# A fused transformer layer on one core: a later square, a later token tile, earlier folds and a reordered bias step

## The chip, the core and the metric

The kernel runs on one core of a Trainium2 chip. Its time is the device time of one execution in microseconds (us). The core's engines are TensorE (PE, matmuls), VectorE (DVE), ScalarE (ACT), GpSimd (POOL) and SyncE (SP, which here only issues DMAs). Each works through its own list of instructions in order and waits on semaphores that the others raise. An instruction that waits holds up all that stand behind it on its engine. ACT also issues DMAs, and these stand in its list between its other instructions.

## The reference

One layer, 1024 tokens of width 1024, all float32:

```
mod = silu(c) @ w_ada + b_ada;  shift1, scale1, gate1, shift2, scale2, gate2 = split(mod, 6)
h = rmsnorm(x, norm1_gain) * (1 + scale1) + shift1
q, k, v, p = split(h @ w_in)                       # 512 | 128 | 128 | 512 columns
attn = sliding_window_attention(q, k, v)           # chunks of 64, window 128, sinks, T5 bias, QK-norm
pool = multiscale_pool(p)                          # causal means over 2, 4, 8, 16 tokens, then a linear map
merged = concat(rmsnorm(attn) * g_a, rmsnorm(pool) * g_p)
x = x + gate1 * (merged @ w_out)
h2 = rmsnorm(x, norm2_gain) * (1 + scale2) + shift2
x = x + gate2 * ((silu(h2 @ w_gate) * (h2 @ w_up)) @ w_down)
```

## The kernel before

Every large product keeps float32 accuracy by splitting both factors into a rounded high part (made by ACT) and a low part (made by DVE): three matmuls stand for one, `mm3` at L2173 to L2175. Tokens lie in eight tiles of 128 (t = 0 to 7), the width in eight blocks of 128 (j = 0 to 7).

**Start.** DVE forms the first modulation vectors from rows of `w_ada`, one instruction of 128x1024 for each block j (L1404): eight columns of `scale1`, eight of `shift1`. ACT makes the gain column from each scale column, then the high parts of the tokens (`h_high_block`) and of `w_in` (`wi_high`); DVE makes the low parts (`h_low_block`, `wi_low`); PE multiplies tiles 0 and 1 with block j (`project_block`). The shift enters as a bias row: ACT and DVE split each shift column (`shift_high` L765, `shift_low` L1553), PE multiplies it with `w_in` (`shift_part`, L2232 and L2233), ACT copies the three finished rows (`shift_row` L780), PE spreads them over 128 partitions (`shift_rows` L2242), and ACT copies them to SBUF (`keep_shift` L785). `evac_q`, `evac_kv` and `evac_p` on DVE (L1564, L1574, L1583) add them to every tile's projections, so nothing of tile 0 leaves PSUM before.

Among these steps ACT squares the token tiles for the RMS norm (`square_x`, L734). Tile t + 1 is loaded into the same buffer `x_st` after the square of tile t, so each square waits for a load of 512 KB. `constants` issues eight small loads on ACT's queue (the bias tiles' source, pool weights, sinks).

**Loop.** `for it in range(NT + 2)` stands on each engine. In turn `it`, PE projects tile `it`, scores belong to tile `it - 1`, and the attention output to tile `it - 2`. A tile from t = 2 on needs `scale_x` (L1534), `h_high` (L746, ACT) and `h_low` (L1541) before its projection.

**Background.** The vectors gate1, scale2 and shift2 come from 24 pieces of 512 KB of `w_ada` (eight for each). SP loads them into a ring of four buffers (`stage`), which lie on the buffers of shift blocks 4 to 7. DVE takes each with one instruction, a fold: L1414 and L1417 for gate1, L1404 for the others. `FOLDS` gives the number for each turn; the ring is refilled as folds end (`ada_used`). `TAKEN` names the turn in which a finished vector is used. The order on each engine is the order of the code; no planner moves it.

After the loop's turns come the output projection and the gated FFN, which no line of the change touches.

Of the kernel before, what the change touches and what calls it, by code (L numbers as in the profile page):

```python
# [26 lines left out]
P = 128  # L27
# [32 lines left out]
def build_program(nc, x, c, w_ada, b_ada, norm1_gain, w_in, q_gain, k_gain, attn_sinks, rel_bias_table,  # L60
                  w_pool, pool_scale, attn_out_gain, pool_out_gain, w_out, norm2_gain, w_gate, w_up,
                  w_down, identity, onehot, inv_count, xt, w_adat, out):
    SEQ, D = x.shape[1], x.shape[2]
    NT = SEQ // P
    KT = D // P
# [11 lines left out]
    RING = 4  # L77
# [10 lines left out]
    with ExitStack() as ctx:  # L88
# [143 lines left out]
        def bank(b):  # L232
            return ps[:, b, :]
# [18 lines left out]
        FOLDS = (3, 4, 4, 5, 4, 4, 0, 0)  # L252
        SCALED = ((), (), (), (), (), (0, 1), (2, 3, 4), (5,), (6, 7))
        TAKEN = {3: GATE1, 4: SCALE2, 6: SHIFT2}
# [243 lines left out]
        def _(sp):  # L498
# [33 lines left out]
            sp.dma_start(g1bc[:, :], b_ada[0, GATE1 * D:(GATE1 + 1) * D].partition_broadcast(P)).then_inc(gate_in, 16)  # L532
            sp.dma_start(g2bc[:, :], b_ada[0, GATE2 * D:(GATE2 + 1) * D].partition_broadcast(P)).then_inc(gate_in, 16)
            sp.wait_ge(hlo_done, KT + 1)
            load_xt(3)
            sp.wait_ge(shift_sum, KT)
            for n, (mm, k) in enumerate(pieces):
                if n >= RING:
                    sp.wait_ge(ada_used, n - RING + 1)
                src = wa_d[k * P:(k + 1) * P, mm * D:(mm + 1) * D] if mm == GATE1 else wat_d[mm * D + k * P:mm * D + (k + 1) * P, :]  # L540
                sp.dma_start(piece_view(n), src).then_inc(stage_in[n % RING], 16)
                if (mm, k) == (GATE1, KT - 1):
                    for j in range(KT // 2):
                        sp.dma_start(wo_raw[:, j, :], wout_d[j * P:(j + 1) * P, :]).then_inc(wo_in[0], 16)
# [141 lines left out]
        def _(act):  # L686
# [122 lines left out]
            shift_high(KT - 4)  # L809
            shift_high(KT - 3)  # L810
            square_x(1)
            for j in range(KT - 2, KT):
                shift_high(j)
            h_high(2)
            constants()
# [49 lines left out]
            for it in range(NT + 2):  # L865
# [65 lines left out]
                if it == 0:  # L931
                    h_high(3)
# [20 lines left out]
                if it + 2 < NT:  # L953
                    square_x(it + 2)
                if 1 <= it and it + 3 < NT:
                    load_xt(it + 3)
# [429 lines left out]
        def _(dve):  # L1386
# [231 lines left out]
            for it in range(NT + 2):  # L1618
# [9 lines left out]
                if it == 0:  # L1628
                    h_low(2)
                    scale_x(3)  # L1630
                    evac_q(0)
# [36 lines left out]
                if it == 0:  # L1668
                    fold(0)
# [35 lines left out]
                if it == 0:  # L1705
                    evac_p(0)
                    dve.wait_ge(wpl_done, 1)
                    evac_q(1)
                    evac_kv(1)
                    bias_tiles()  # L1710
                    h_low(3)
                    fold(1)
# [17 lines left out]
                if 1 <= it < NT - 1:  # L1730
                    evac_q(it + 1)
                if it < NT:
                    for n in range(sum(FOLDS[:it]) if it else 2, sum(FOLDS[:it + 1])):
                        fold(n)
                    if it < NT - 1:
                        scale_wo(it)
# [433 lines left out]
        def _(pe):  # L2170
# [19 lines left out]

            pe.wait_ge(vrow_in, 16 * 2)
# [52 lines left out]
            def project_first():  # L2244

                for j in range(KT - 1):
                    project_block(0, j)
                    project_block(1, j)
                    if j == 1:
                        small_vectors()  # L2250
                    if j >= 4:
                        if j == 4:
                            pe.wait_ge(vcol_done, 2)
                            pe.wait_ge(rel_done, 1)
                        for part in range(3):
                            shift_part(part, (j - 4,))
                project_block(0, KT - 1)
                project_block(1, KT - 1, (1,))
# [5 lines left out]
                project_block(1, KT - 1, (0, 2))  # L2264
# [420 lines left out]
```

## Time and profile before

| | us |
|---|---|
| median of 3 runs | 962.2 (962.1 to 962.76) |
| the profiled execution | 962.17 |
| its span, first to last instruction | 960.4 |
| PE busy, of the span | 925.4 (96%) |
| DVE busy | 789.3 (82%) |
| ACT busy | 521.0 (54%) |
| POOL busy | 283.8 (30%) |

The page lists for each engine the time in which it works. The chain of waits is followed back from the last instruction, at each step to what let it start. A timeline row gives an instruction's start and length, and in brackets the idle time of the engine before it with what ended that. The busy share is a mean over very different stages, so the stages are read one by one.

### The profile page before, as it was taken

The page shows a single profiled execution, that of the slowest core. Times are in us where ns is not written, and L with a number is a line of the kernel's source. Part 1 is how long each engine was busy: PE and PEld are TensorE (multiplying, and loading weights), DVE is VectorE, ACT ScalarE, POOL GpSimd, SP SyncE. Part 2 cuts the span into 40 slices and gives each one's busy share as a digit, 9 for nine tenths or more (in the row PEclk, how much of TensorE's full clock was granted, in tenths as well). Part 3 has the DMA queues.
Part 4 walks back from the last instruction along what each step waited for, and adds up shares of the span by engine and source line. Part 5 has one row for each costly group of instructions (what it writes and reads, how often), then busy time and mean ns, then how long its engine had stood idle before and what let it go on. Part 6 is the DMA issues. An engine that isn't in the chain of part 4 may idle for free.

```text
span 960.4 us, 14014 instructions
## 1 busy us (share of the span) xinstructions
PE 925.4 (96%) x4327; PEld 760.3 (79%) x4327; DVE 789.3 (82%) x1239; ACT 521.0 (54%) x1006; POOL 283.8 (30%) x243
## 2 busy tenths in 40 slices
PE   7988999989999998999999999999999999999998
PEld 6647788778887777888888888888888888888886
DVE  4949999999689968888787977879698787977797
ACT  4544655576345645555464654646465464655543
POOL 0025455432100100703306061240704215070334
PEclk9999999999999999999999999999999999999999
DMA  9965754338345495557456556644656556455624
GB/s 359 390 214 158 281 176 154 110 122 274 132 129 179 142 328 209 197 202 259 152 195 227 210 178 218 220 173 175 227 198 231 196 186 229 175 183 210 219 88 176
DMA packets 96135, 193.97 MB, mean 202 GB/s; under 512 B 6512, under 2 KB 57440, under 8 KB 96096
## 3 DMA queue, kind: packets, MB, share of 16 engines
q1 hardware_dynamic: 90816, 182.05, 54.2%
q10 hardware_dynamic: 5280, 11.45, 3.3%
q8 instruction: 19, 0.31, 0.1%
q14 instruction: 20, 0.16, 0.1%
HBM read 176.30 MB, written 17.17 MB: 201 GB/s over the span
## 4 chain that ended last, share of the span: by engine, by line
PE 71%; DVE 17%; issue 4%; DMA 3%; ACT 3%; POOL 1%; SPq 1%; ACTq 0%; DVEq 0%; POOLq 0%
PE ps L2173 23%; PE ps L2174 23%; PE ps L2175 23%; DVE stage L1404 2%; DMA raw_u<-in_w_up 1%; DVE wo_raw L1500 1%; DVE ada_in_raw L1404 1%; DMA x_st<-in_x 1%; DVE nmax L1645 1%; DMA wi_raw<-in_w_in 1%; DVE acc L1417 1%; DVE s_sb L1644 1%; DVE wi_lo L1588 1%; DVE wo_lo L1505 1%; PE ps L2426 1%
## 5 line engine op out<-in xcount | busy, mean ns | idle before, releaser
L1348 POOL TENSOR_TENSOR x<-x,p1s 128x512 f32<-128x512 f32 x80 | 117.0, 1483 | 422.4 <-ACT p1s L1045 421.6
L2173 PE MATMUL ps<-bs,ring 128*128 128x512 f32 x344 | 134.2, 390 | 3.3 <-ACT ps L973 2.6
L2175 PE MATMUL ps<-bs,ring 128*128 128x512 f32 x344 | 133.9, 389 | 0.0
L2174 PE MATMUL ps<-bs,ring 128*128 128x512 f32 x344 | 133.8, 389 | 0.0
L1787 DVE TENSOR_TENSOR ring<-s,ring 128x512 fp32r<-128x512 f32 x88 | 68.7, 799 | 50.0 <-ACT ring L966 50.0
L2173 PE MATMUL ps<-h_hi,ring 128*128 128x512 f32 x272 | 106.1, 390 | 0.6 <-DVE h_lo L1780 0.6
L2174 PE MATMUL ps<-h_lo,ring 128*128 128x512 f32 x272 | 105.8, 389 | 0.0
L2175 PE MATMUL ps<-h_hi,ring 128*128 128x512 f32 x272 | 105.8, 389 | 0.0
L966 ACT ACTIVATE ring<-s 128x512 fp32r<-128x512 f32 x88 | 53.8, 623 | 66.5 <-PE ps L2175 66.5
L2173 PEld LDWEIGHTS ps<-bs,ring 128*128 128x128 f32 x344 | 64.6, 188 | 18.1 <-issue 3.4
L2173 PE MATMUL ps<-wi_hi,ht_hi 128*128 128x512 f32 (+1 forms) x192 | 71.0, 370 | 7.9 <-DVE ht_lo L1547 2.3
L2175 PEld LDWEIGHTS ps<-bs,ring 128*128 128x128 f32 x344 | 64.6, 188 | 13.4
L2174 PEld LDWEIGHTS ps<-bs,ring 128*128 128x128 f32 x344 | 64.6, 188 | 13.3
L2174 PE MATMUL ps<-wi_lo,ht_hi 128*128 128x512 f32 (+1 forms) x192 | 68.7, 358 | 0.0
L2175 PE MATMUL ps<-wi_hi,ht_lo 128*128 128x512 f32 (+1 forms) x192 | 68.5, 357 | 0.0
L2173 PEld LDWEIGHTS ps<-h_hi,ring 128*128 128x128 f32 x272 | 51.1, 188 | 11.5 <-DVE h_lo L1780 1.0
L2175 PEld LDWEIGHTS ps<-h_hi,ring 128*128 128x128 f32 x272 | 51.1, 188 | 10.6
L2174 PEld LDWEIGHTS ps<-h_lo,ring 128*128 128x128 f32 x272 | 51.1, 188 | 10.5
L2173 PE MATMUL ps<-wo_hi,h_hi 128*128 128x512 f32 x128 | 51.3, 401 | 0.8 <-DVE x L1526 0.5
L2174 PE MATMUL ps<-t_lo_d,h_hi 128*128 128x512 f32 x132 | 51.4, 389 | 0.0
L1845 DVE TENSOR_TENSOR x<-x,ps 128x512 f32<-128x512 f32 x40 | 26.4, 681 | 29.4 <-PE ps L2175 29.4
L2173 PEld LDWEIGHTS ps<-wi_hi,ht_hi 128*128 128x128 f32 x192 | 36.8, 191 | 17.1 <-issue 5.0
(302 smaller groups left out, 2344.2 us busy)
## 6 DMA issues: line engine op xcount, KB each, us to landing
bs<-bs_scratch SPq DMA_DIRECT2D x166, 512.0 KB, 6.2
raw_g<-in_w_gate SPq DMA_DIRECT2D x11, 1024.0 KB, 5.3
raw_u<-in_w_up SPq DMA_DIRECT2D x11, 1024.0 KB, 7.7
raw_d<-in_w_down SPq DMA_DIRECT2D x20, 512.0 KB, 4.2
ada_in_raw<-in_w_adat SPq DMA_DIRECT2D x16, 512.0 KB, 11.1
stage<-in_w_adat SPq DMA_DIRECT2D x16, 512.0 KB, 5.7
wi_raw<-in_w_in SPq DMA_DIRECT2D x8, 640.0 KB, 12.3
stage<-in_w_ada SPq DMA_DIRECT2D x8, 512.0 KB, 4.6
```

The source lines that it names most:

```text
L966: act.activation(ring[m][(par + pos(p, o)) % 2][:, 0], a_source(m, o), ACT.Copy).then_inc(a_hi, 1)
L1348: pool.tensor_tensor(x1_half(t, 1), x1_half(t, 1), p1s[j][:, :], ALU.add).then_inc(pool_evac, 1)
L1404: return dve.scalar_tensor_tensor(out=piece, in0=piece, scalar=1.0, in1=row, op0=ALU.mult, op1=ALU.mult, accum_out=mod_sum[:, v, j:j + 1])
L1417: ins = dve.scalar_tensor_tensor(out=acc[:, :], in0=piece_view(n), scalar=cact[:, 0, k:k + 1], in1=acc[:, :], op0=ALU.mult, op1=ALU.add)
L1500: dve.scalar_tensor_tensor(out=wo_raw[:, k, :], in0=wo_raw[:, k, :], scalar=gmix[:, k:k + 1], in1=g1bc[:, :], op0=ALU.mult, op1=ALU.mult). ...
L1505: dve.tensor_tensor(wo_lo[:, k, :], wo_raw[:, k, :], wo_hi_row(k).bitcast(F32), ALU.subtract).then_inc(wo_lo_done, 1)
L1588: dve.tensor_tensor(wi_lo[:, j, cols], wi_raw[:, j, cols], wi_hi[:, j, cols].bitcast(F32), ALU.subtract).then_inc(wi_lo_done, 1)
L1787: dve.tensor_tensor(r[:, 1], a_source(m, o), r[:, 0].bitcast(F32), ALU.subtract).then_inc(a_lo, 1)
L1845: dve.tensor_tensor(c, c, bank(XB[j]), ALU.add).then_inc(down_evac, 1)
L2173: pe.matmul(dst, s_hi, m_hi, start=start, stop=False, skip_group_check=onto)
L2174: pe.matmul(dst, s_hi, m_lo, start=False, stop=False, skip_group_check=onto)
L2175: return pe.matmul(dst, s_lo, m_hi, start=False, stop=stop, skip_group_check=onto)
```

## The change

- ACT squares tile 1 after the last four shift columns and after `h_high(2)`, ahead of `constants`; before, it stood between shift columns 5 and 6.
- The low and high parts of tile 3 are made in turn 1 and not in turn 0: `scale_x(3)` and `h_low(3)` on DVE stand around turn 1's folds, `h_high(3)` on ACT behind turn 1's `square_x(3)`.
- Three gate1 folds stand ahead of `evac_q(0)`; before, one stood behind the `v` copies of turn 0 and two between the bias tiles and the first scores. Turn 1 has three folds instead of four, turn 5 has five instead of four, and scale2 is taken in turn 5.
- SP loads piece n (0 to 3) as soon as shift column 4 + n is done; before, all four waited for column 7. The two gate rows `g1bc` and `g2bc` are loaded after the first fold and not ahead of token tile 3.
- PE fills its wait after block 0 with eight matmuls on a matrix of ones, into a bank that nobody reads then. The last k and v block of tile 1 stands behind the shift products and not ahead of them.

```diff
-        FOLDS = (3, 4, 4, 5, 4, 4, 0, 0)
+        FOLDS = (3, 3, 4, 5, 4, 5, 0, 0)
-        TAKEN = {3: GATE1, 4: SCALE2, 6: SHIFT2}
+        TAKEN = {3: GATE1, 5: SCALE2, 6: SHIFT2}
...
             load_xt(2)
-            sp.dma_start(g1bc[:, :], b_ada[0, GATE1 * D:(GATE1 + 1) * D].partition_broadcast(P)).then_inc(gate_in, 16)
-            sp.dma_start(g2bc[:, :], b_ada[0, GATE2 * D:(GATE2 + 1) * D].partition_broadcast(P)).then_inc(gate_in, 16)
             sp.wait_ge(hlo_done, KT + 1)
             load_xt(3)
-            sp.wait_ge(shift_sum, KT)
             for n, (mm, k) in enumerate(pieces):
-                if n >= RING:
+                if n < RING:
+                    sp.wait_ge(shift_sum, KT - RING + n + 1)
+                else:
                     sp.wait_ge(ada_used, n - RING + 1)
+                if n == RING:
+                    for bc, gate in ((g1bc, GATE1), (g2bc, GATE2)):
+                        sp.dma_start(bc[:, :], b_ada[0, gate * D:(gate + 1) * D].partition_broadcast(P)).then_inc(gate_in, 16)
...
             square_x(0)
-            shift_high(KT - 4)
-            shift_high(KT - 3)
-            square_x(1)
-            for j in range(KT - 2, KT):
+            for j in range(KT - 4, KT):
                 shift_high(j)
             h_high(2)
+            square_x(1)
             constants()
...
-                if it == 0:
-                    h_high(3)
...
                 if it + 2 < NT:
                     square_x(it + 2)
+                if it == 1:
+                    h_high(3)
...
                 if it == 0:
                     h_low(2)
-                    scale_x(3)
+                    fold(0)
+                    fold(1)
+                    fold(2)
                     evac_q(0)
...
-                if it == 0:
-                    fold(0)
...
                     bias_tiles()
-                    h_low(3)
-                    fold(1)
...
                     evac_q(it + 1)
+                if it == 1:
+                    scale_x(3)
                 if it < NT:
-                    for n in range(sum(FOLDS[:it]) if it else 2, sum(FOLDS[:it + 1])):
+                    for n in range(sum(FOLDS[:it]) if it else 3, sum(FOLDS[:it + 1])):
                         fold(n)
+                    if it == 1:
+                        h_low(3)
...
+            def keep_busy_gap(n):
+                for _ in range(n):
+                    pe.matmul(bank(6)[:, 0:P], ones[:, :], ones[:, :], start=True, stop=True)
...
                     project_block(1, j)
+                    if j == 0:
+                        keep_busy_gap(8)
...
                 project_block(0, KT - 1)
-                project_block(1, KT - 1, (1,))
                 for j in (KT - 5, KT - 4):
...
-                project_block(1, KT - 1, (0, 2))
+                project_block(1, KT - 1, (1, 0, 2))
```

ACT, end of the start phase, before: the squares (`x_st,ssx`), the shift columns (`sh`) and the high part of tile 2 (`ht_hi<-sq_m`), up to the first copied shift row.

```order
L734 ACTIVATE x_st,ssx<-x_st 128x1024
L737 DMA x_st<-in_x 128x1024
L765 ACTIVATE sh<-mod_sum,vcol 128x1 x2
L734 ACTIVATE x_st,ssx<-x_st 128x1024
L737 DMA x_st<-in_x 128x1024
L765 ACTIVATE sh<-mod_sum,vcol 128x1 x2
L746 ACTIVATE ht_hi<-sq_m 128x1024
L718 DMA bias<-rel_scratch 64x4x128 x2
```

The same place of the changed kernel, whose line numbers are two higher.

```order
L736 ACTIVATE x_st,ssx<-x_st 128x1024
L739 DMA x_st<-in_x 128x1024
L767 ACTIVATE sh<-mod_sum,vcol 128x1 x4
L748 ACTIVATE ht_hi<-sq_m 128x1024
L736 ACTIVATE x_st,ssx<-x_st 128x1024
L739 DMA x_st<-in_x 128x1024
L720 DMA bias<-rel_scratch 64x4x128 x2
```

The second square now stands behind four shift columns and behind tile 2's high part; it still stands ahead of the constants and of every shift row.

ACT, from turn 1 to turn 2, changed kernel: the exponentials and square of turn 1, the high part of tile 3 (`ht_hi<-xs`), then turn 2's copies of pool output (`mT`), probabilities (`pt_sb`) and queries (`qbd`).

```order
L841 ACTIVATE sinkex<-sinkin 128x4
L736 ACTIVATE x_st,ssx<-x_st 128x1024
L739 DMA x_st<-in_x 128x1024
L748 ACTIVATE ht_hi<-xs 128x1024
L743 DMA xs<-in_xt 128x1024
L879 ACTIVATE mT<-ps 128x512
L821 ACTIVATE pt_sb<-ps 128x512 x2
L898 ACTIVATE qbd<-ps,vcol 64x8x64 x2
```

The row `ht_hi<-xs` is new here; before, it stood in turn 0 behind the square of q and k, so all of turn 2 now stands behind it.

DVE, end of turn 1, as a piece of the difference: tile 2's q leaves PSUM (L1564), then the folds into `acc`, then k and v of tile 2 (L1574) and the next scores.

```order
 L1583 SCALAR_TENSOR_TENSOR p_sb<-ps,rsx,bp 128x512
 L1564 SCALAR_TENSOR_TENSOR qkv<-ps,rsx,bqkv 128x512
-L1417 SCALAR_TENSOR_TENSOR acc<-stage,cact,acc 128x1024 x4
+L1534 TENSOR_TENSOR xs<-xs,a 128x1024
+L1417 SCALAR_TENSOR_TENSOR acc<-stage,cact,acc 128x1024 x3
+L1541 TENSOR_TENSOR ht_lo<-xs,ht_hi 128x1024
 L1574 SCALAR_TENSOR_TENSOR qkv<-ps,rsx,bqkv 128x256
```

Two instructions on tile 3 come in around the folds, and one fold leaves.

## Rows read from the trace of the kernel before

**Rows 1.** The chain of waits, shares of the span by engine

```profile
PE 71%; DVE 17%; issue 4%; DMA 3%; ACT 3%; POOL 1%; SPq 1%; ACTq 0%; DVEq 0%; POOLq 0%
```

**Rows 2.** By stage: length, busy PE, PEld, DVE, ACT, POOL, PE clock, DMA share, GB/s

```profile
16.30:19.00 2.70, 2.69 (x8) 2.30 (x9) 1.71 (x4) 1.53 (x3) 0.00 (x0) 0.50 1.01 409
...
30.00:45.00 15.00, 14.62 (x76) 10.86 (x75) 15.00 (x26) 8.41 (x15) 1.85 (x2) 1.00 1.01 381
...
75.00:195.00 120.00, 110.10 (x640) 94.44 (x640) 116.39 (x236) 71.53 (x204) 59.25 (x57) 0.99 0.52 176
...
400.00:800.00 400.00, 400.00 (x1766) 331.20 (x1765) 320.68 (x464) 218.59 (x379) 121.44 (x86) 1.00 0.57 204
```

**Rows 3.** Timeline (start us, length us, [idle before]) of PE, block 1 of tiles 0, 1

```profile
16.32 0.79 PE L2173 MATMUL ps<-wi_hi,ht_hi 128*128 128x512 f32 x1 [2.33 <-DVE ht_lo L1547]
...
19.63 0.39 PE L2173 MATMUL ps<-wi_hi,ht_hi 128*128 128x512 f32 x1
...
21.45 0.23 PE L2206 MATMUL ps<-ident,mT 18*128 18x18 f32 x1
```

**Rows 4.** Timeline of DVE, start phase

```profile
24.34 0.48 DVE L1547 SCALAR_TENSOR_TENSOR ht_lo<-xs,a,ht_hi 128x256 fp32r<-128x256 f32 x1 [2.91 <-ACT ht_hi L761]
...
37.27 1.23 DVE L1404 SCALAR_TENSOR_TENSOR ada_in_raw<-ada_in_raw,crow 128x1024 f32<-128x1024 f32 x1
...
46.72 1.23 DVE L1404 SCALAR_TENSOR_TENSOR ada_in_raw<-ada_in_raw,crow 128x1024 f32<-128x1024 f32 x1
...
52.34 0.22 DVE L1553 SCALAR_TENSOR_TENSOR sh<-mod_sum,vcol,sh 128x1 fp32r<-128x1 f32 x1 [4.38 <-ACT sh L765]
...
61.22 0.75 DVE L1564 SCALAR_TENSOR_TENSOR qkv<-ps,rsx,bqkv 128x512 f32<-128x512 f32 x1 [4.05 <-ACT bqkv L785]
```

**Rows 5.** DMA issued at 20.42: size, us to landing

```profile
ada_in_raw<-in_w_adat SPq DMA_DIRECT2D x1, 512.0 KB, 15.4
```

**Rows 6.** Timeline of ACT, end of the start phase (ACTq: its DMA issues)

```profile
50.43 1.06 ACT L734 ACTIVATE x_st<-x_st 128x1024 f32<-128x1024 f32 x1 [4.70 <-DMA x_st<-in_x]
...
52.01 0.67 ACT L765 ACTIVATE sh<-mod_sum,vcol 128x1 fp32r<-128x1 f32 x2 [0.43 <-ACT x_st L734]
53.73 1.06 ACT L746 ACTIVATE ht_hi<-sq_m 128x1024 fp32r<-128x1024 f32 x1 [1.05 <-DVE sq_m L1534]
...
56.88 1.31 ACTq L727 DMA_DIRECT2D sinks<-in_attn_sinks  x2
58.24 0.59 ACT L780 ACTIVATE shrow_q<-ps 2x512 f32<-2x512 f32 x1 [3.46 <-PE ps L2233]
```

**Rows 7.** Timeline of PE: shift products, shift rows, scores of tiles 0 and 1

```profile
53.88 0.59 PE L2232 MATMUL ps<-wi_hi,sh 128*2 128x512 f32 x1 [0.64 <-DVE sh L1553]
...
59.34 1.12 PE L2242 MATMUL ps<-shrow_q,ones 2*128 2x512 f32 x2
...
71.95 1.95 PE L2400 MATMUL ps<-kT,qbd 128*128 128x128 f32 x16
...
91.69 2.02 PE L2400 MATMUL ps<-kT,qbd 128*128 128x128 f32 x16 [1.10 <-ACT kT L848]
```

**Rows 8.** Timeline of DVE, turns 0 and 1

```profile
71.36 2.08 DVE L1541 TENSOR_TENSOR ht_lo<-xs,ht_hi 128x1024 fp32r<-128x1024 f32 x1
73.37 3.50 DVE L1417 SCALAR_TENSOR_TENSOR acc<-stage,cact,acc 128x1024 f32<-128x1024 f32 x2
76.80 0.68 DVE L1644 TENSOR_TENSOR s_sb<-ps,bias 128x512 f32<-128x512 f32 x1
...
88.22 6.14 DVE L1417 SCALAR_TENSOR_TENSOR acc<-stage,cact,acc 128x1024 f32<-128x1024 f32 x4
...
94.67 0.68 DVE L1644 TENSOR_TENSOR s_sb<-ps,bias 128x512 f32<-128x512 f32 x1
```

**Rows 9.** Timeline of ACT, the first copy of turn 2

```profile
85.78 0.60 ACT L879 ACTIVATE mT<-ps 128x512 f32<-128x512 f32 x1 [2.66 <-PE ps L2300]
```

**Rows 10.** Timeline of POOL, the pool weights

```profile
67.92 1.27 POOL L1332 TENSOR_TENSOR wpl<-wpl,pt_sb 128x512 f32<-128x512 f32 x1
```

## The prediction

> **What bounds the kernel now.** I read the chain of waits first. Over the span it is 71% PE and 17% DVE [rows 1], so the question is which stages are DVE's. The busy time by stage tells: from 400 to 800 us PE works all 400.00 us, while from 30 to 45 DVE works 15.00 of 15.00 and from 75 to 195 it works 116.39 of 120 against PE's 110.10 [rows 2]. The reader is to see that the change lies wholly in DVE's stages. What DVE gains there before the loop ends starts PE's long stage sooner by as much; nothing behind it is touched. The timelines then show three places where DVE waits or is late.
>
> - PE comes to block 1 at 16.32 after 2.33 us idle and runs it at half its clock: the granted clock is 0.50 from 16.3 to 19.0 [rows 2, 3]. DVE waits 2.91 at 24.34 for what follows from that block [rows 4].
> - DVE has formed the last shift column at 46.72 + 1.23 = 47.95, and then waits 4.38 for ACT's shift column 6, which stands behind the square of tile 1, which waited 4.70 for its load [rows 4, 6]. DVE waits 4.05 more for the bias row, until 61.22 [rows 4].
> - The first scores are ready on PE from 71.95, but DVE adds their bias only at 76.80, behind the low part of tile 3 and two folds [rows 7, 8].
>
> All times below count from the start of the trace before. Its execution took 962.17, that is the span of 960.4 and 1.8 around it, and lies 0.03 under the median of 962.2.
>
> **A, the eight filling matmuls (gain 1.4).** Nine matmuls of tile 0 took 19.63 - 16.32 = 3.31 us at half clock. The same nine of tile 1, at full clock, took 21.45 - 19.63 = 1.82 with the small wait behind them [rows 3]. So 1.5 is to be had. The eight become 16 instructions of the form of the scores, which take 1.95 / 16 = 0.12 each [rows 7]: 1.95 of the 2.33 idle, 0.4 left. At half clock they would take 3.9 and make the block 1.6 late; the blocks ahead of the gap had no such wait, so I count this a rival and not a bound. From block 1 the way goes over ACT's small vectors to DVE's 24.34, and DVE has no idle time from 30 to 45 [rows 2], so the gain reaches 47.95. One load limits it: the scale column of block 7 was issued at 20.42, landed 15.4 later at 35.8 and was used at 37.27 [rows 4, 5]. That leaves 1.4. Bounds: 0 and 1.5.
>
> **B, the square behind the shift columns (gain 2.2).** Without the wait for the load, shift column 6 can be split at 47.95. Before, tile 2's high part on ACT began 53.73 - 52.34 = 1.39 after that [rows 4, 6], so now at 49.3; it ends at 50.4. The square of tile 1 finds its load at 50.43, as before, and with its accumulator read and the next load's issue takes 52.01 - 50.43 = 1.6 [rows 6]. The constants' issues take from 53.73 to 56.88 + 1.31 = 58.19, 4.5 us [rows 6], so they end at 56.5, and the shift row's copy, 0.59, ends at 57.1. On PE the shift products can now run through from about 49.5; what lay between 53.88 and 59.34 takes at most 5.5, so PE is done by 55 and waits 2.1. ACT, with the square and the constants ahead of the row, is what is late next. PE spread the row at 59.34 [rows 7], now at 57.1. B keeps A only if the square's load also comes 1.4 sooner. It is issued 1.4 sooner, and the two gate rows, 1 MB or 2.6 us at the 409 GB/s of the start [rows 2], are no longer ahead of it, so I take A whole. Bounds: 1.1, if PE spreads the first row at half clock (1.12 more), and 2.5. The k and v block behind the shift products costs nothing, since PE has 2 us to spare there.
>
> **C, the folds and tile 3 out of the way of the first scores (gain 3.9).** From `evac_q(0)` to the scores on PE it is 71.95 - 61.22 = 10.7 us, and half of the 16 score matmuls, 1.0, make the first chunk. DVE came 76.80 - 61.22 = 15.6 after `evac_q(0)` [rows 4, 7, 8]. Now 11.7: 3.9 sooner. DVE no longer ends this stretch, PE does. Bounds: 0 and the 2.08 + 3.50 = 5.6 that leave DVE [rows 8]. The three folds lie in the wait before `evac_q(0)`: low part of tile 2 until about 51.7, then 0.75 + 2 x 1.23, by 55.0, against an `evac_q(0)` at 59.0 without A. Their pieces are issued when shift columns 4 to 6 end, by 46.72 at the latest [rows 4]; with the 8 us that the square's load took they are there by 54.7, so even the last leaves 3 us. `scale_x(3)`, 1.2, leaves the same wait, which is why it counts below.
>
> **D, tile 3 in turn 1 (loss 2.75).** This is the price. `h_high(3)` on ACT stands ahead of all copies of turn 2, and waits for `scale_x(3)`, which stands on DVE behind `evac_q(2)`. That ended at 88.22; DVE's next scores began at 94.67, 6.45 later [rows 8]. Now: `scale_x(3)` 1.2, `h_high(3)` 1.06, then turn 2's chain over ACT and PE from the `mT` copy to the scores, 91.69 - 85.78 = 5.9 [rows 7, 9], and 1.0 for the first chunk: 9.2. DVE's own work in that time, one scale, three folds and a low part, 5 x 1.23 = 6.2, lies within it. Loss 9.2 - 6.45 = 2.75. Bounds: 1.9, if the copies of the probabilities no longer wait for PE, and 4.2, if all PE work of the chain runs at half clock.
>
> DVE's own 6.2 stands on 1.23 for each [rows 4]. Before, beside POOL's window sums, the four folds took 6.14, 1.53 each, and the low part of tile 3 took 2.08 [rows 8]; five at 2.08 would be 10.4, past the 9.2, and the loss 4.0. I take 1.23, because POOL's sums of tile 1 start only after ACT's copy of its projection, which is now behind the five.
>
> By the Trainium skill, page "SBUF — State Buffer", section "SBUF: two separate sides", a VectorE instruction with two SBUF inputs and a GpSimd instruction that reads SBUF lock each other out of a shared port. By that rule the loss is 2.75, since POOL has nothing to do then; by the mean of 1.53, taken for these forms everywhere, it would be the same, and only at 2.08 each 4.0. The trace agrees with the rule in so far as these forms are slow only beside POOL.
>
> **E, the fifth fold in turn 5 (loss 1.25).** One fold of 1.23 more where DVE is full [rows 2]; beside POOL up to 2.1 [rows 8]. The scale2 step only moves from turn 4 to 5.
>
> **At no cost:** the earlier pieces (SP waits for shift columns instead of the last one, and its next item was piece 0 anyway) and the later gate rows, first used in turn 3.
>
> Sum: 1.4 + 2.2 + 3.9 - 2.75 - 1.25 = 3.5, so 962.17 - 3.5 = **958.7**. Likely own range 957.8 to 959.9.
>
> **The rivals.**
>
> *PE loses its clock.* PE idles 2.1 us ahead of the shift row, and in turn 2 the `mT` copy comes 88.22 + 2.26 = 90.5 instead of 85.78, so PE waits 4.7 more there. After 2.33 idle PE was slow at 16.32, and after a wait of 0.64 that followed another one it was slow at 53.88 [rows 3, 7]. Against it: the first of the new idles is shorter than 2.33. Price: B 1.1 less and D 1.45 more, 961.2.
>
> *The loads on ACT's queue come late.* The gate rows and pieces 4 to 6 now fall on the time of the constants. POOL scaled the pool weights at 67.92 without waiting for them [rows 10]; POOL and the constants' issue both come some 3.5 sooner, so they meet as before unless the DMAs are slower. The gate rows alone are 2.6 us of DMA time; between none and all of that is lost, 1.5 as a middle: 960.2, at worst 961.3. By the Trainium skill, page "DMA: Bandwidth & Descriptors", section "Queues, rings and completion order", each DMA engine takes packets in turn from the queues that have work for it, so that SP's loads slow ACT's; by that rule this rival is the likelier. The square's load, for which ACT waited 4.70, fits it [rows 6].
>
> *The fillers don't hold the clock.* A is 0: 960.1. Little speaks for it; the idle left is 0.4.
>
> *More than the sum.* D lies at its lower bound, 1.9, and the fifth fold falls into a wait of DVE in turn 5, so E is 0: 956.6. For it, DVE is busy 116.39 of 120, not all [rows 2]; against it, those 3.6 are split over six turns.
>
> *Slower: ACT's queue holds turn 2.* The other terms make 6.25, so the gain is gone once the stretch after `evac_q(2)` takes 6.45 + 6.25 = 12.7. That needs PE to fall behind DVE too: right after the scores PE projects tile 3's q, 24 matmuls of about 0.23 or 5.5 us, and if turn 2's copies have to wait for all of that, 9.2 + 5.5 = 14.7 make the kernel 2.0 slower: 964.2. Against it: PE is idle 9.9 us from 75 to 195 and can catch up [rows 2].
>
> **How the numbers follow.** Forecast 0.60, clock 0.12, late loads 0.10, fillers 0.05, more 0.08, slower 0.05. What a measurement of this kernel can tell from no change is about 0.2%, 1.9 us. Faster, under 960.3: forecast, more, fillers and half of the late loads are 0.78, less 0.03 for the forecast's own tail: 0.75. Within: clock, the other half of the loads, and 0.02 of that tail: 0.19. Slower: 0.06. The range, 957.1 to 961.3, takes in clock, loads and fillers, and leaves out the slower case and most of the case of more.
>
> **What would show it.** A: the granted clock stays at 1 from 16 to 20 and DVE's 24.34 becomes 22.9. B: no idle of DVE before the second part of shift column 6, and the shift row's copy directly behind the constants. C: first bias add within 1.2 us of the first scores. D: an idle time of about 3 us on DVE before the second tile's scores, ended by PE, behind ACT's `h_high(3)`. E: five folds in turn 5, DVE without idle. The prediction is wrong if the gain up to the first scores, 7.5 us, is not there, or if DVE's wait in turn 2 is under 1 or over 5 us.

## The result, and the profile after

| | before | changed |
|---|---|---|
| median of 11 runs each, us | 961.86 (960.78 to 962.76) | 966.17 (962.49 to 967.02) |
| ratio, 95% interval | | 1.0035 [1.0023, 1.0048] |
| the profiled execution, its span, us | 962.17, 960.4 | 962.49, 960.7 |

The changed kernel is 0.35% slower by the ratio, which is estimated over all runs of both; the two medians lie 0.45% apart. Forecast was 958.7, with a range up to 961.3. The profiled execution is the fastest of the changed kernel's eleven, so this trace shows less than the whole loss; the experiments bring a second one nearer the median.

The chain of waits by engine, which answers to [rows 1]:

```profile
PE 78%; DVE 12%; DMA 4%; ACT 3%; issue 2%; ACTq 1%; SPq 0%; POOL 0%; DVEq 0%; POOLq 0%
```

PE has seven points more and DVE five fewer. The stages of the same trace, columns as in [rows 2]:

```profile
13.60:18.00 4.40, 3.96 (x27) 3.46 (x27) 3.03 (x4) 2.05 (x5) 0.00 (x0) 1.00 1.01 412
...
52.00:56.00 4.00, 1.34 (x6) 0.75 (x4) 1.84 (x2) 0.00 (x0) 0.00 (x0) 1.00 0.91 275
56.00:60.00 4.00, 2.12 (x5) 1.24 (x6) 0.00 (x0) 1.92 (x4) 0.00 (x0) 0.83 1.03 338
60.00:64.00 4.00, 4.00 (x8) 2.05 (x7) 2.04 (x4) 2.54 (x5) 0.00 (x0) 0.50 1.04 374
...
84.00:88.00 4.00, 0.04 (x1) 0.07 (x2) 3.90 (x4) 2.21 (x4) 0.00 (x0) 0.74 0.30 80
88.00:92.00 4.00, 4.00 (x15) 3.53 (x16) 3.16 (x4) 2.62 (x5) 0.77 (x2) 0.50 0.89 308
184.00:188.00 4.00, 2.70 (x6) 2.17 (x7) 3.86 (x8) 2.81 (x15) 0.21 (x1) 0.62 0.00 0
400.00:800.00 400.00, 400.00 (x1767) 331.16 (x1765) 320.12 (x464) 218.41 (x378) 122.19 (x85) 1.00 0.58 205
```

The long stage is as it was. The granted clock (the last column but two; 1.00 is 2.4 GHz, 0.50 is 1.2) is 1.00 where it had been 0.50, at block 1. Three places show the lower level: around 60, from 88 and around 185. Only the third has no counterpart in the kernel before, whose clock is 1.00 there. The first two are longer than what stood there before, of which these are the rows:

```profile
52.00:56.00 4.00, 2.74 (x11) 1.06 (x12) 2.67 (x5) 1.65 (x3) 0.00 (x0) 0.71 1.01 392
56.00:60.00 4.00, 4.00 (x15) 2.06 (x14) 1.18 (x2) 1.33 (x3) 0.00 (x0) 0.86 0.93 241
...
84.00:88.00 4.00, 4.00 (x20) 3.70 (x21) 3.86 (x11) 1.71 (x3) 0.34 (x1) 0.57 0.73 262
```

In the changed kernel the first two stand right behind a stretch in which PE hardly worked. PE's timeline shows the waits (columns as in [rows 3]); it answers to [rows 3] and [rows 7]:

```profile
13.66 1.95 PE L2195 MATMUL ps<-ones 128*128 128x128 f32 x16
16.04 0.50 PE L2175 MATMUL ps<-wi_hi,ht_hi 128*128 128x512 f32 x1 [0.44 <-DVE ht_lo L1547]
...
57.88 1.36 PE L2248 MATMUL ps<-shrow_q,ones 2*128 2x512 f32 x2 [4.54 <-ACT shrow_q L782]
59.05 2.76 PE L2248 MATMUL ps<-shrow_kp,ones 2*128 2x256 f32 x4
...
71.86 2.02 PE L2407 MATMUL ps<-kT,qbd 128*128 128x128 f32 x16
...
87.96 1.09 PE L2360 MATMUL ps<-ident,qn 128*128 128x128 f32 x4 [4.95 <-ACT pt_sb L821]
...
93.21 2.02 PE L2407 MATMUL ps<-kT,qbd 128*128 128x128 f32 x16
```

What PE waits for is ACT, both times. ACT's timeline, which answers to [rows 6] and [rows 9]:

```profile
50.70 1.36 ACTq L720 DMA_DIRECT2D bias<-rel_scratch  x2
52.11 1.01 ACTq L723 DMA_DIRECT2D pt_sb<-in_inv_count  x1
53.15 0.60 ACTq L724 DMA_DIRECT2D wpl<-in_w_pool  x1
53.78 2.04 ACTq L725 DMA_DIRECT2D pt_sb<-in_pool_scale  x1
55.85 1.35 ACTq L729 DMA_DIRECT2D sinks<-in_attn_sinks  x2
57.25 0.59 ACT L782 ACTIVATE shrow_q<-ps 2x512 f32<-2x512 f32 x1 [6.97 <-issue]
...
61.85 0.60 ACT L787 ACTIVATE bp<-ps 128x512 f32<-128x512 f32 x1 [1.32 <-PE ps L2248]
62.34 0.73 ACT L775 ACTIVATE sq_qk<-qkv 128x640 f32<-128x640 f32 x1
...
85.79 1.06 ACT L748 ACTIVATE ht_hi<-xs 128x1024 fp32r<-128x1024 f32 x1 [6.34 <-DVE xs L1534]
...
86.75 0.58 ACT L879 ACTIVATE mT<-ps 128x512 f32<-128x512 f32 x1
```

The constants' issues took 6.50 us (50.70 to 57.20); the forecast took 4.5 from [rows 6]. In turn 2 ACT stands 6.34 us for tile 3. DVE's timeline, which answers to [rows 4] and [rows 8]:

```profile
22.63 0.48 DVE L1547 SCALAR_TENSOR_TENSOR ht_lo<-xs,a,ht_hi 128x256 fp32r<-128x256 f32 x1 [1.47 <-ACT ht_hi L763]
...
45.65 1.22 DVE L1404 SCALAR_TENSOR_TENSOR ada_in_raw<-ada_in_raw,crow 128x1024 f32<-128x1024 f32 x1
...
60.01 0.75 DVE L1564 SCALAR_TENSOR_TENSOR qkv<-ps,rsx,bqkv 128x512 f32<-128x512 f32 x1 [6.07 <-ACT bqkv L787]
...
73.09 0.69 DVE L1646 TENSOR_TENSOR s_sb<-ps,bias 128x512 f32<-128x512 f32 x1 [1.89 <-PE ps L2407]
...
83.88 0.74 DVE L1564 SCALAR_TENSOR_TENSOR qkv<-ps,rsx,bqkv 128x512 f32<-128x512 f32 x1
...
94.37 0.69 DVE L1646 TENSOR_TENSOR s_sb<-ps,bias 128x512 f32<-128x512 f32 x1 [3.11 <-PE ps L2407]
```

It is ahead of the kernel before by 1.07 at the last shift column, 1.2 at the first q, 3.7 at the first bias add, and 0.3 at the second. So the forecast's 7.5 up to the first scores is half missing, and turn 2 takes what came.

### The profile page after: what moved, and what is told of

Read it like the earlier page. It is cut to its first block, busy times and chain, and to the rows that moved or that the text cites. A ratio compares the mean times of both kernels' runs of the same rounds, so it can differ in the third digit from the quotient of the medians.

```text
span 960.7 us, 14046 instructions
## 1 busy us (share of the span) xinstructions
PE 928.3 (97%) x4343; PEld 763.5 (79%) x4343; DVE 785.4 (82%) x1239; ACT 520.6 (54%) x1006; POOL 277.5 (29%) x243
## 4 chain that ended last, share of the span: by engine, by line
PE 78%; DVE 12%; DMA 4%; ACT 3%; issue 2%; ACTq 1%; SPq 0%; POOL 0%; DVEq 0%; POOLq 0%
PE ps L2175 25%; PE ps L2177 24%; PE ps L2176 24%; DMA ada_in_raw<-in_w_adat 2%; DMA raw_u<-in_w_up 1%; DVE stage L1404 1%; DVE ada_in_raw L1404 1%; PE ps L2296 1%; PE ps L2407 1%; DMA wi_raw<-in_w_in 1%; DVE wo_lo L1505 1%; PE ps L2433 1%; ACT ht_hi L748 0%; DVE xs L1534 0%; DVE wi_lo L1588 0%
## 5 line engine op out<-in xcount | busy, mean ns | idle before, releaser
L2176 PEld LDWEIGHTS ps<-bs,ring 128*128 128x128 f32 x344 | 64.6, 188 | 13.1
L2177 PE MATMUL ps<-wo_hi,h_lo 128*128 128x512 f32 x128 | 50.0, 390 | 0.0
```

Source lines behind the costliest of these rows:

```text
L2176: pe.matmul(dst, s_hi, m_lo, start=False, stop=False, skip_group_check=onto)
L2177: return pe.matmul(dst, s_lo, m_hi, start=False, stop=stop, skip_group_check=onto)
```

## The experiments

My theory after this: ACT's queue holds PE twice. The constants' issues stretch because the loads that the early folds release fall on them, and tile 3's high part holds turn 2; behind each wait PE runs at the lower clock. Rivals: the gate rows stretch the issues, turn 2 or the fifth fold alone decides, the clock at the start is paid back later. Ratios are to runs of the kernel before on the same chip, so variants from different chips are compared by their ratios; that of the changed kernel is 1.0035, and 1.0038 in e8.

### e1: the fillers alone

In the kernel before:

```diff
+                    if j == 0:
+                        keep_busy_gap(8)
```

> The kernel before with the eight filling matmuls alone (term A). If the fillers do what was forecast, the granted clock stays at 1 from 16 to 20 us, the last shift column ends 1.1 to 1.4 us sooner (46.6 to 46.9 instead of 47.95), and of that at most 1.4 is left at the end: 960.5 to 961.9. If the gain is lost because the shift row still stands behind the square and its load, the time is that of the kernel before within 0.3. If a full clock at the start is paid for by a fall of the granted clock later (the rival), a new stretch at 0.50 shows after 50 us and the time is above 963.

Measured: 959.86 against 961.18, ratio 0.9989 [0.9981, 0.9998]. A gain of about 1.1 (0.2 to 1.8), so A is real by the times. The profiled execution took 961.63, 1.8 above the median, and in it the gain does not pass the shift row. The last shift column ends at 46.59, 1.36 sooner, but the load of the second square, issued 1.36 sooner, lands only 0.2 sooner, so the shift row's copy is 0.26 sooner (57.98). PE then ran the shift products at the lower clock for longer: the granted clock is 0.88, 0.50 and 0.76 in the windows from 48 to 60, against 1.00, 0.71 and 0.86 before. The first q comes at 61.50, no sooner than before. So the second of the expectation's cases is what this trace shows; no stretch at the lower clock is new, but this one is longer.

### e2: tile 3's scale and high part back in turn 0

```diff
+                    scale_x(3)
                     evac_q(0)
...
-                if it == 1:
-                    scale_x(3)
...
+                if it == 0:
+                    h_high(3)
...
-                if it == 1:
-                    h_high(3)
```

> The changed kernel with tile 3's scale and high part back in turn 0 (the scale behind the three folds in the wait for the shift row, the high part on ACT behind the first square of q and k); its low part stays in turn 1 behind the folds. If ACT's wait for tile 3 is what holds turn 2 (term D and the half clock behind it), ACT's copies of turn 2 start at the end of evac of q of tile 2, PE's idle of about 5 us from 83 to 88 and the 0.50 from 88 to 92 are gone, and the kernel is 3 to 4 us faster than the changed one: 962 to 963. If PE's late start in turn 2 has another cause (the rival: DVE's folds and low part), PE is idle there as before and the gain is under 1 us.

Measured: 962.56, ratio 1.0013 [1.0002, 1.0025]: the time is in the expected band, but by the ratios the gain over the changed kernel is 0.22%, about 2 us and not 3 to 4. From the q of tile 2 to the second bias add it takes 95.34 - 88.24 = 7.10; in the kernel before 94.67 - 87.56 = 7.11, in the changed one 94.37 - 83.88 = 10.49. The clock stays at 1.00 from 84 to 96. So tile 3's scale and high part, for which ACT waits, make the whole of D. But in this profile the issues took 8.1 us and PE waited 6.36 for the shift row.

### e3: the gate rows in their old place

```diff
             load_xt(2)
+            sp.dma_start(g1bc[:, :], b_ada[0, GATE1 * D:(GATE1 + 1) * D].partition_broadcast(P)).then_inc(gate_in, 16)
+            sp.dma_start(g2bc[:, :], b_ada[0, GATE2 * D:(GATE2 + 1) * D].partition_broadcast(P)).then_inc(gate_in, 16)
```

The same two lines are gone from the loop over the pieces.

> The changed kernel with the loads of the two gate rows back in their old place on SP's queue, ahead of tile 3's tokens. If it is these rows that stretch the issue of ACT's constants from 4.46 to 6.5 us, the issues take 4.5 again, the shift row's copy starts at about 55.2 instead of 57.25, PE's idle ahead of it is 2.5 instead of 4.54 us, and the kernel is 1 to 2 us faster than the changed one. If the pieces do it, or the square's load now waits for the gate rows, the shift row comes no sooner and the time is that of the changed kernel within 0.5.

Measured: 966.56, ratio 1.0060 [1.0046, 1.0075]. No gain. ACT's second square and its last issues in this run:

```profile
50.45 1.06 ACT L735 ACTIVATE x_st<-x_st 128x1024 f32<-128x1024 f32 x1 [1.42 <-DMA x_st<-in_x]
...
54.63 1.50 ACTq L724 DMA_DIRECT2D pt_sb<-in_pool_scale  x1
56.17 4.44 ACTq L728 DMA_DIRECT2D sinks<-in_attn_sinks  x2
60.66 0.59 ACT L781 ACTIVATE shrow_q<-ps 2x512 f32<-2x512 f32 x1 [9.06 <-issue]
```

With the gate rows gone from there the eight issues took 8.6 us, and the two for the sinks, 1 KB each, 4.44 instead of 1.31. So the gate rows are not needed for the stretch; whether they add to it in the changed kernel is not shown. The expectation's other case came too: behind the gate rows the square's load is late, the square starts at 50.45 instead of 49.15, and the issues at 52.02 instead of 50.70. So the later gate rows brought the square forward, as B had it.

### e4: the constants behind the kept shift rows

```diff
             square_x(1)
-            constants()
...
                     keep_shift(2)
+                    constants()
```

> The changed kernel with ACT's constants issued behind the three kept shift rows instead of ahead of the shift row's copy. If the issues on ACT's queue hold the shift row and the half clock behind PE's idle eats A and B, the copy starts when PE is done with the products (about 53.5 instead of 57.25), PE idles under 1.5 us, the granted clock from 56 to 68 is at least 0.9, DVE's first q comes at about 57 instead of 60.01, and the kernel is 3 to 4 us faster than the changed one, unless the pool weights or the bias tables then come late: in that case POOL's scaling of the weights (67.8) or DVE's bias tiles move back by 2 to 4 us and the gain is gone. If the idle there decides nothing (the rival: turn 2 decides), the time is that of the changed kernel within 1.

Measured: 964.31, ratio 1.0033 [1.0021, 1.0045]: by the ratio no gain over the changed kernel, which the expectation's exception and its rival both allow. The trace tells them apart. The first q came at 55.32, 4.7 sooner than in the changed kernel, but the second q at 69.30 instead of 69.10:

```profile
69.30 0.75 DVE L1564 SCALAR_TENSOR_TENSOR qkv<-ps,rsx,bqkv 128x512 f32<-128x512 f32 x1 [2.59 <-POOL wpl L1332]
```

POOL's weights take the place of the shift row, as the exception had it: the issues now stand ahead of `square_qk(0)`, and POOL waits 1.56 us for the last of these loads before it scales the weights at 68.00. One thing I did not expect: PE passed from the products to the rows at 53.44 with no wait over 0.4, and its clock fell all the same, to 0.50 from 57 to 60, which makes 0.62 of this stretch:

```profile
56.00:60.00 4.00, 3.78 (x10) 2.99 (x11) 0.47 (x2) 0.48 (x1) 0.00 (x0) 0.62 0.97 368
```

### e5: the later pieces wait for the shift rows

```diff
                 if n == RING:
+                    sp.wait_ge(shift_done, 3)
```

> The changed kernel with one wait more on SP's queue: the gate rows and the fourth and later GATE1 pieces are issued only when the shift rows are kept. If the loads that the early folds release are what stretches the issue of ACT's constants (6.5 us in the changed kernel, 8.1 and 8.6 in two of its variants, 4.4 to 4.5 with the old order), the issues take 4.5 us again and land in about 5 instead of 10, the shift row's copy starts at about 55.2, PE idles 2 to 2.5 us ahead of it as forecast in B, and the kernel is 2 to 4 us faster than the changed one: 962 to 964. If the first three pieces, loaded before 48 us, do it (the rival), the issues stay at 6 us or more and so does the time.

Measured: 961.41, ratio 0.9999 [0.9990, 1.0009]: the loss is gone with one wait, but the gain that was forecast is not there. ACT's timeline:

```profile
53.26 0.53 ACTq L726 DMA_DIRECT2D pt_sb<-in_pool_scale  x1
53.82 1.44 ACTq L730 DMA_DIRECT2D sinks<-in_attn_sinks  x2
55.31 0.59 ACT L783 ACTIVATE shrow_q<-ps 2x512 f32<-2x512 f32 x1 [5.00 <-issue]
```

The eight issues take 4.53 us (50.73 to 55.26) and the copy comes at 55.31. The loads too land sooner. The DMA view (KB each, median us to landing) has for the pool scale, first in the changed kernel, then here:

```profile
pt_sb<-in_pool_scale ACTq DMA_DIRECT2D x1, 256.0 KB, 11.1
```

```profile
pt_sb<-in_pool_scale ACTq DMA_DIRECT2D x1, 256.0 KB, 4.7
```

With e3, where the gate rows were gone and the issues stretched all the same, this points to the three pieces that the early folds release, 1.5 MB on SP's queue between 52 and 56.

### e6: the constants among the shift columns

```diff
-            for j in range(KT - 4, KT):
+            for j, loads in zip(range(KT - 4, KT), (bias_loads, pool_loads, scale_load, sink_loads)):
                 shift_high(j)
+                loads()
             h_high(2)
             square_x(1)
-            constants()
```

(the four functions are `constants` cut in parts)

> The changed kernel with the issues of ACT's constants put one or two at a time behind shift columns 4 to 7, in ACT's waits of about 1 us there, so that nothing but the second square stands ahead of the shift row. If ACT's issues are what holds the shift row, its copy starts when PE is done (53 to 54), PE has no idle there and keeps its clock, the constants land before 58 and hold nothing, and the kernel is 5 to 7 us faster than the changed one: 959 to 961. If the issues are stretched there too, the shift columns come late instead, by 2 us or more, and the gain is under 3. If turn 2 decides everything (the rival), the first scores come 5 us sooner and the time does not change.

Measured: 959.80, ratio 0.9982 [0.9973, 0.9991], 4.8 under the changed kernel on the same chip (e8). The copy of the shift row starts at 53.74 and PE waits 1.22 for it instead of 4.54; but the sinks' two issues, right behind SP's first four pieces, took 4.04 us and held `h_high(2)`:

```profile
47.07 4.04 ACTq L734 DMA_DIRECT2D sinks<-in_attn_sinks  x2
```

The time is the expected one, but not the "hold nothing": an issue is stretched there too, with none of the later pieces issued yet. PE did not keep its clock either: it is at 0.50 from 57 to 62, behind waits of 1.22 and 0.66.

### e7: the folds of the turns as before

```diff
-        FOLDS = (3, 3, 4, 5, 4, 5, 0, 0)
+        FOLDS = (3, 4, 4, 5, 4, 4, 0, 0)
-        TAKEN = {3: GATE1, 5: SCALE2, 6: SHIFT2}
+        TAKEN = {3: GATE1, 4: SCALE2, 6: SHIFT2}
```

> The changed kernel with the folds of the turns as before (four in turn 1 and four in turn 5, the scale2 step in turn 4); three stay in the wait for the shift row. If the fifth fold is what costs term E, the turn of tile 5 is 1.1 to 1.25 us shorter, and the stretch at a low granted clock from 184 to 192, which no trace with the old folds has, is gone with 0.5 to 1 us more: 964.2 to 964.8. The fourth fold of turn 1 lies in DVE's wait of 3.11 us there and costs nothing. If turn 5 has room (the rival), there is no gain; if DVE's work decides in turn 2, it is 1.2 us slower.

Measured: 963.26, ratio 1.0020 [1.0010, 1.0030], 1.4 under the changed kernel on the same chip (e8), with intervals that overlap. The stretch at the lower clock around 186 is gone:

```profile
184.00:188.00 4.00, 2.33 (x11) 1.61 (x10) 3.74 (x8) 3.13 (x12) 0.00 (x0) 1.00 0.01 2
```

That the new folds always bring this stretch is not so: e5, which has them, shows 1.00 from 172 to 196, although PE waits 2.43 us there as in the changed kernel (2.38).

### e8: the changed kernel once more

> The changed kernel once more, for a second profile. Its one profile so far is of its fastest run, 3.7 us under its median. If the run to run difference comes from the constants' issue, a profile of a run near the median shows these issues at 8 us or more instead of 6.5, the shift row's copy at 59 to 61 instead of 57.25 and the stretch at half clock behind it longer by about as much; if it comes from elsewhere, 57.25 stands and another place is late.

Measured: 964.63, ratio 1.0038 [1.0025, 1.0051]; the profiled execution took 964.58. Its ACT timeline:

```profile
53.36 1.50 ACTq L725 DMA_DIRECT2D pt_sb<-in_pool_scale  x1
54.89 3.06 ACTq L729 DMA_DIRECT2D sinks<-in_attn_sinks  x2
58.00 0.59 ACT L782 ACTIVATE shrow_q<-ps 2x512 f32<-2x512 f32 x1 [7.60 <-issue]
```

The issues took 7.1 us, under the 8 that I expected. The copy is 0.75 later than in the first profile, the first q 1.47 later (61.48), the second bias add 1.75 later (96.12) and the span 2.1 longer. So neither number of the expectation came, but the direction holds: 0.75 of the later first q is the issues, 0.7 the first row, which PE ran in 2.07 us instead of 1.36 at the lower clock, and 0.35 of the difference in the span arises behind the second bias add.

### e9: e2 and e5 together

> The changed kernel with two of the former edits together: the later pieces wait for the kept shift rows, and tile 3's scale and high part are back in turn 0. If the two causes are independent (the issues of the constants 2 to 3 us, turn 2 about 3.5 us), the issues take 4.5 us, DVE's first scores are added at about 71.5 and its second ones 17.9 after them as in the kernel before (94.67 - 76.80), at about 90 instead of 94.67, and the time is 957 to 958.5, which is the forecast of 958.7. If the gain from one eats that of the other (the rival: PE falls behind in turn 2), it is 960 or more.

Measured: 956.89, ratio 0.9957 [0.9945, 0.9970], 1.8 under the forecast, which had D's loss in it (without D it is 956.0). DVE's first bias add, q of tile 2, second bias add:

```profile
70.75 0.69 DVE L1648 TENSOR_TENSOR s_sb<-ps,bias 128x512 f32<-128x512 f32 x1 [2.01 <-PE ps L2407]
...
81.54 0.74 DVE L1565 SCALAR_TENSOR_TENSOR qkv<-ps,rsx,bqkv 128x512 f32<-128x512 f32 x1
...
88.64 0.67 DVE L1648 TENSOR_TENSOR s_sb<-ps,bias 128x512 f32<-128x512 f32 x1
```

It is 6.0 us ahead of the kernel before at all three, where e5 is 1.5 ahead at the last. The two gains add up, and neither eats the other.

### e10: fillers in turn 2

```diff
                     pe.wait_ge(qkn_done, a + 1)
+                    if it == 2:
+                        pe.wait_ge(q_evac, 2)
+                        for _ in range(18):
+                            pe.matmul(bank(0)[:, 0:P], ones[:, :], ones[:, :], start=True, stop=True)
```

> The changed kernel with 18 more filling matmuls (128 by 128, into a bank that is free there) on PE in turn 2, behind the probabilities' transposes, where it waits 4.95 us for ACT. They take about 4.4 us. If the half clock behind that wait is what makes D larger than the forecast, the granted clock stays at 1 from 84 to 96, the chain from the first copy of the probabilities to the scores takes 1 to 1.5 us less, and the kernel is 1 to 1.5 us faster than the changed one: 963 to 964. If the wait alone makes D (the rival), the time does not change.

Measured: 963.99, ratio 1.0028 [1.0017, 1.0038]. PE and the clock in turn 2:

```profile
85.75 4.29 PE L2360 MATMUL ps<-ones 128*128 128x128 f32 x36 [0.35 <-DVE kn L1702]
90.26 0.66 PE L2364 MATMUL ps<-ident,qn 128*128 128x128 f32 x4 [0.23 <-ACT pt_sb L821]
```

```profile
88.00:92.00 4.00, 3.77 (x31) 3.49 (x30) 3.79 (x4) 3.54 (x6) 0.00 (x0) 1.00 0.67 212
```

The clock stays at 1.00, and from the q of tile 2 to the second bias add it takes 95.57 - 86.27 = 9.30, against 10.53 in e8 and 7.11 before. So D is 2.2 at the full clock and 3.4 at half: the clock is 1.2 of it. In the run's time it does not show: the ratio is not told apart from the changed kernel's, and the issues in this profile took 8.0 us.

### e11 and e12: all four edits, and three of them

e11 joins e2, e5, e6 and e7; e12 is e11 without e6.

> The changed kernel with all four edits: the later pieces wait for the kept shift rows, the constants are issued behind shift columns 4 to 7, tile 3's scale and high part are in turn 0, and the folds of turns 1 and 5 are as before. If the causes add up, the shift row's copy starts when PE is done (about 53.5), the first scores are added near 69.5 (7 us ahead of the kernel before), nothing is lost in turn 2 or in the turn of tile 5, and the time is 954 to 956, 6 us under the kernel before. If PE's half clock in turn 0 or POOL's weights take the place of the shift row (the rival), the first scores come at 71 or later and the time is 957 or more.

> The changed kernel with three edits: the later pieces wait for the kept shift rows, tile 3's scale and high part are in turn 0, and the folds of turns 1 and 5 are as before; the constants stay ahead of the shift row. If term E (1.1 us) and the stretch at a low granted clock from 176 to 184 that the same kernel with the new folds shows are what is left of the loss, it is 1 to 2 us faster than with two edits (956.89): 955 to 956. If the fourth fold in turn 1 now holds the second scores (the rival: there DVE no longer waits for PE, since tile 3's work is out of ACT's way), the second scores come 1.2 us later after the q of tile 2 than with two edits, and the time is the same within 0.5.

Measured: e11 956.64, ratio 0.9950 [0.9937, 0.9963]; e12 958.13, ratio 0.9963 [0.9950, 0.9977]. Neither is told apart from e9 by its interval, and both miss their first numbers. In e12 the rival held: the fourth fold of turn 1 now stands ahead of the second bias add.

```profile
82.40 6.13 DVE L1418 SCALAR_TENSOR_TENSOR acc<-stage,cact,acc 128x1024 f32<-128x1024 f32 x4
88.45 1.91 DVE L1542 TENSOR_TENSOR ht_lo<-xs,ht_hi 128x1024 fp32r<-128x1024 f32 x1
```

From the q of tile 2 to that add it takes 90.68 - 81.74 = 8.94 instead of e9's 7.10, which gives back what the fifth fold had cost; e11 has the same 8.94 (90.09 - 81.15). e9 and e11 are 0.4 to 0.5% under the kernel before and so beat both.

## Why the prediction was wrong

Where DVE stands against the kernel before, in us (minus is sooner), from the profiled executions:

| | first q | second q | first bias add | second bias add | k, v of tile 6 | span |
|---|---|---|---|---|---|---|
| before, start | 61.22 | 69.22 | 76.80 | 94.67 | 181.42 | 960.4 |
| forecast | -3.6 | | -7.5 | -4.75 | -3.5 | -3.5 |
| changed | -1.2 | -0.1 | -3.7 | -0.3 | +0.3 | +0.3 |
| changed again (e8) | +0.3 | +1.3 | -2.0 | +1.5 | +2.1 | +2.4 |
| e5 | -2.7 | -1.6 | -5.3 | -1.5 | -0.9 | -1.2 |
| e9 | -3.7 | -2.6 | -6.0 | -6.0 | -5.3 | -5.8 |

**The step that failed** first is in B: "The constants' issues take from 53.73 to 56.88 + 1.31 = 58.19, 4.5 us [rows 6], so they end at 56.5". With it falls "At no cost: the earlier pieces". A time of the old order was carried into an order in which other loads fall on the same stretch. In the changed kernel's profiles and the variants that keep the early pieces and the issues' place the eight issues took 6.5 to 8.6 us; without the early pieces 4.4 to 4.5 (e5, e9, e12). e8's span missed the forecast by 5.9 us. e5, which mends this step alone, is ahead of e8 by 2.9 at the second bias add and by 3.6 at the end (it also lacks the fall of the clock around 186). The other 2.3 are still there in e5: 0.9 at the first q, 1.3 in C and 1.0 in D, less 0.9 in what follows. The rival on late loads had the right cause, SP's loads beside ACT's, but I looked for its effect where the data are used (POOL's weights) and not on the engine that issues, and priced it at 961.3 at worst.

By the Trainium skill, page "DMA: Bandwidth & Descriptors", section "Queues, rings and completion order", the DMA engines alternate between the queues that have work, so that SP's loads slow ACT's; the traces agree (11.1 us to landing against 4.7 in e5). Section "Issuing engines are not separate DMA queues" of that page calls the time that an engine spends on starting a DMA usually small beside the transfer. Here it is not always: in e3 the two loads of 1 KB took 4.44 us to issue, and landed 9.3 us (median) after it.

**A** held at its place (22.63 where 22.9 was forecast) and reached the last shift column with 1.07 of 1.4; DVE waits 0.31 for a load on the way. e1's times give about 1.1.

**B** at the issues' old length is nearly right: in e5 the row's copy comes at 55.31, and by the working 56.5 less A's 1.4 is 55.1. That PE spreads the row as soon as ACT's copy ends held too (55.95 in e5, the copy ends at 55.90). What remains is the clock, which I had only as a bound: PE ran this row in 1.79 us in e5, against 1.12 before [rows 7].

**C** was seen (the first bias add is 1.23 us behind the scores), but from the first q to that add it takes 13.1 to 13.3, not 11.7. PE's k, v and p rows at half clock took 2.76 instead of 1.45 us, ACT's square of q and k stands behind their copies, and the second q came 9.1 after the first instead of 8.0.

**D** cost 3.4, not 2.75: 2.2 at full clock, 1.2 for the clock (e10). Its mechanism came as forecast: DVE waits 3.11 for PE, behind ACT's `h_high(3)`. DVE's own work went without POOL, as assumed: tile 3's low part took 1.22, and 2.16 beside POOL's sums in e2. The rival "PE loses its clock" was right and had 1.45 and 1.1 as its prices for D and B. The first measured 1.2. For the second no run holds the clock alone; in the changed kernel the first row is 0.24 longer and ACT's square of q and k comes 2.33 behind the first q instead of 1.25. Its counterargument, that the first idle is shorter than 2.33, does not hold: the idle was 4.54, and in e9, where it was 2.23, the clock fell to 0.50 as well.

**E** cost 1.13 at its place (the offset goes from -0.8 at 170 to +0.3 at 182, and e8 has the same). The fall of the clock around 186, which was in no step, is on top where it comes; e7's median gives 1.4 for both, with intervals that overlap.

In sum for e8, against the forecast: 3.9 at the first q, 1.6 up to the first bias add, 0.7 in turn 2, less 0.3 in what follows, that is from -3.5 to +2.4. What the changed kernel's runs at 966 to 967 us look like was not profiled; e3, at 966.99 with issues of 8.6 us, is the nearest. Open is also why an issue takes longer: the runs show that it does when SP has just issued large loads, not which part of issuing waits. That the lower clock in turn 0 follows from PE's wait alone is not so: in e4 it fell without one, so a shorter wait ahead of the row need not keep it.

## What to carry to other kernels

In these runs the length of a DMA issue was not a constant of the engine that issues (4.4 to 8.6 us for the same eight): before moving loads on one queue, look at what other engines issue in that stretch, and at what computes behind those issues. A wait that holds background loads until a critical copy is done can be worth more than the early load (here 0.4%). Before work is moved into a later turn, ask which engine has it at the head of its list there. On DVE the low part in the place of one fold cost nothing (7.10 from the q of tile 2 to the second bias add in e2, 7.11 before), with four folds beside it 1.8 (e12); the one high part on ACT cost 3.4.

## What was not expected of the hardware

- SP's own issues stretch too: the three later pieces took 3.83 us to issue in the changed kernel, against 1.80 for the first four in the kernel before. In e6 a single gate row took 3.42, from 54.60 on, when ACT's eight had been issued by 51.11.
- PE's granted clock fell to its lower level at 57 in e4 although PE worked on; ahead of that it had run the shift products (2 columns), nine full matmuls and the rows (2 partitions).
